# A decay step deferred by half a unit in GLA, and the gates' tanh issued behind the next weight split

## The chip, the core and the metric

One Trainium2 chip, one of its NeuronCores. The metric is the device time of one execution of the whole program in microseconds; lower is better. The program is one launch, hand-scheduled for the five engines: TensorE (PE), VectorE (DVE), ScalarE (ACT), GpSimd (POOL) and SyncE (SP, which issues the weight DMAs).

## What is computed

Two transformer-like blocks in fp32 on a sequence of 512 tokens of width 1024. The first is a hybrid layer: an mLSTM mixer with an output gate, three groups of dilated attention, two merge gates, a SwiGLU FFN. The second has a gated linear attention (GLA), an NSA mixer (compressed, selected and window attention), two merge gates and an FFN. Cut to what the change touches:

```python
# first block
y_a = sigmoid(o_pre) * hm                                # om: 8 column tiles of o_pre
g_a, g_b = split(sigmoid(gate_pre), 2)                   # ga, gb
merged = g_a * (y_a @ w_proj_a) + g_b * (y_b @ w_proj_b) # pa, pb
# second block, GLA (4 heads of 128, chunks of 64)
log_a = log_sigmoid(a_lr @ w_alpha2 + b_alpha) / 16
b = cumsum(log_a)                    # inside each chunk
qe = q * exp(b);  ke = k * exp(-b);  kd = k * exp(b_last - b)
o = ...                              # scores, states over chunks, rms norm
o = o * silu(r)                      # gr: 8 column tiles of r
# merge
mixed = sigmoid(merge_gla) * (o_gla @ w_proj_gla) + sigmoid(merge_nsa) * (o_nsa @ w_proj_nsa)
#                  mg                    pg                    mn                    pn
```

## The kernel before

All projections are cut into 320 "units" in one fixed order (`UNITS`): a unit is a 128-column tile of a weight matrix, up to 8 blocks of 128 x 128 deep. Its weights arrive by a DMA of 512 KB into one of three buffers RAW. For fp32 accuracy each weight is split into a high and a low part: ACT writes WH (L1416, a Copy to fp32r), and then DVE writes WL = RAW - WH (L1695), or POOL does (L2299) where the unit's index is odd and its name is in `BUSY_DVE` (`lo_on_pool`). PE then makes 24 matmuls of 512 columns (L1043 to L1045: high x high, high x low, low x high for each of 8 blocks), about 5.4 us for a unit. WH and WL have three buffers too, so the split of unit u+3 may start when PE is done with unit u.

The order is written out by hand in Python functions that every engine runs with its own class (`Sync`, `Tensor`, `Scalar`, `Vector`, `Pool`), so each engine's instructions come in the order of the same calls:

- `ahead(e, i)`, at a unit's start, issues `split(i + 2)` and `load(i + 5)`.
- `unit(e, i)`: `ahead`, half the products, `flush`, the other half, `flush`, `evict`. `Fill` does the same by quarters (`quarter`; a flush after the second and the fourth) and puts the quarters between the steps of an attention stage: in NSA 96 quarters of the 24 units mg, pg and mn are spread over 28 items, about two of them ahead of an item's scaling and one behind it. Between an item's quarters and the next stand `ask` (PE's scores L1325 or L1337; DVE's L2191 and maximum L2198; ACT's Exps L1614), the output of the item before (PE L1369) and the turn (PE's transposes L1347, ACT's L1625 and DVE's L2252 copies).
- `evict(e, i)`: DVE scales the unit's sum by the row norm (`scaled`, L1723; for gk L1804 and L1806, for gq L1796, for pg L1751). For the gates om, ga, gb, mg, mn (L1438) and gr (L1441) ACT then applies tanh in place or to `th2`. It appends the unit to the list `e.later`.
- `flush(e)` takes each entry of `e.later` once: for a gate DVE turns tanh into the sigmoid (L1852, an SBUF to SBUF TENSOR_SCALAR) or into silu (L1863, for gr); for token-ordered tiles (gv, gk and others) PE transposes the evicted tile (L1108) and DVE copies it out (L1882).

A GLA head's decay is also worked off through `e.later`, as `("decay", h, p)`: p = 0 is the cumulative sum on DVE (L2089) and two Exps on ACT (L1581, L1582); p = 1 four DVE instructions (L2093, L2095, L2099, L2100) and an Exp (L1585); p = 2 one DVE multiply (L2103). Decay 0 starts in the flush in the middle of gr1, decay 1 in that of gv2, decay 2 in that of gv4 and decay 3 in that of gk2. gq waits for "eb" and gk for "enb" and "ekd" of its head. Between heads stands `gla_turned` (PE: scores L1248, transposes L1286 of the head before, updates L1261; DVE: masked copy L2113, gated products L2144, states L2123 and L2126), then `gla_outs` and `gla_scaled` (L2135). `final_norm` (L2107) is one DVE instruction in each of 8 flushes from gv4 on. The order of GLA's units is gr0, gr1, gq0, gk0, gv2, gv3, gq1, gk1, gv4, gv5, gq2, gr2, gr3, gk2, gv6, gv7, gq3 and so on.

DVE, ACT and PE each work strictly in their own order, so an instruction that waits holds all that stand behind it on its engine.

Of the kernel before, what the change touches and what calls it, by code (L numbers as in the profile page):

```python
# [46 lines left out]
def unit_order():  # L47
# [58 lines left out]
    for j in range(8):  # L106
# [8 lines left out]
UNITS = unit_order()  # L115
AT = {(n, j, k0): i for i, (n, j, k0, nk) in enumerate(UNITS)}
PARTS = {"qm": 2, "km": 2, "vm": 1, "om": 1, "va": 1, "ga": 1, "gb": 1, "pb": 1, "small2": 1, "gk": 1, "gv": 1,
         "gr": 1, "vs": 1, "vw": 1, "mg": 1, "mn": 1, "pn": 1}
TOKENS = ("vm", "va", "gk", "gv", "vs", "vw", "small2")
SB = [2, 3, 4]  # L120
OB = 5
# [48 lines left out]
class Order:  # L170
# [3 lines left out]
    def __init__(self):  # L174
        self.ring, self.taken, self.turn = [0, 1, 2, 3], 0, 0
        self.holder, self.bank, self.before, self.later = {}, {}, {}, []
        self.turns_apart = False

    def hold(self, bank, *key):
        self.bank[key], self.before[key] = bank, self.holder.get(bank)  # L180
# [10 lines left out]
    def none(self, *a):  # L191
        pass

    start = load = split = products = evict = after = fold = spread = none
    ones = gates_1 = gates_2 = bias_vector = store_vectors = gate_columns = none
    spread_max = scores = weights = numerators = normed = gated = split_ya = none
    enter_attention = load_bias = attention_scores = attention_softmax = attention_turn = attention_out = none
# [47 lines left out]
            flush_all(self.e)  # L245


def flush(e, turns=True):

    for _ in range(len(e.later)):  # L250
        what, i, part = e.later.pop(0)
        if what == "unit":
            name = UNITS[i][0]
            if name in TOKENS and part == 1:
                if not turns:
                    e.later.append((what, i, part))
                    continue
                e.turn_bank("tokens", i)
            e.after(i, part)
            if part < PARTS.get(name, 1):  # L260
                e.later.append(("unit", i, part + 1))
        elif what == "decay":
            e.decay(i, part)
            if part < 2:
                e.later.append(("decay", i, part + 1))
        elif what == "log_sigmoids":
            e.log_sigmoids_end()
            e.decay(0, 0)
            e.later.append(("decay", 0, 1))
        elif what == "yg":  # L270
            e.split_yg(i)
        elif what == "final":
            e.final_norm(i)
            if i < 7:
                e.later.append(("final", i + 1, 1))
# [7 lines left out]
def ahead(e, i):  # L283
    if i + 2 < len(UNITS):
        e.split(i + 2)
    if i + 5 < len(UNITS):
        e.load(i + 5)

# [9 lines left out]

def evict(e, i):
    e.evict(i)  # L300
    if UNITS[i][0] in PARTS or UNITS[i][:1] + UNITS[i][2:3] == ("down", 16):
        e.later.append(("unit", i, 1))

# [426 lines left out]
def build(nc, xT_d, wst_d, con_d, col_d, relb_d, oh_d, wa2_d, w1_d, w2_d, out_d, scr_d):  # L730
# [6 lines left out]
    with ExitStack() as ctx:  # L737
# [28 lines left out]
        def at(*name):  # L766
            return reached[name] if counted else reached.get(name, (None, 0))
# [615 lines left out]
        class Scalar(Order):  # L1383
# [43 lines left out]
            def two_spreads(s):  # L1427
# [2 lines left out]
                t = A.activation(R1, PS[:, s.bank["spread", "n4"], :], ACT.Copy, scale=1.0)  # L1430
                t.then_inc(*act_done["norm"].next("free", "spread", "n4"))

            def evict(s, i):
                name, j, k0, nk = UNITS[i]
                if name in ("om", "ga", "gb", "mg", "mn"):
                    act.wait_ge(*at("free", "sum", i))
                    x = gate_tile(i)
                    A.activation(x, x, ACT.Tanh, scale=0.5).then_inc(*act_done["attn"].next("tanh", i))  # L1438
                elif name == "gr":
                    act.wait_ge(*at("free", "sum", i))  # L1440
                    t = A.activation(th2, rr[:, j % 2 * 512:j % 2 * 512 + 512], ACT.Tanh, scale=0.5)  # L1441
                    t.then_inc(*act_done["attn"].next("tanh", i))
                elif name == "small2":
                    act.wait_ge(*at("free", "sum", i))
                    t = A.activation(gts[0:24, :], gts[0:24, :], ACT.Tanh, scale=0.5)
                    t.then_inc(*act_done["attn"].next("tanh", i))
                elif name == "out":
                    act.wait_ge(*at("free", "sum", i))
                    s.scaled_hi("h2", AH, j, XT[:, j, :], col("ffn_g", j))
                    s.square("n2", j, XT[:, j, :])  # L1450
                elif name in ("gate", "gate2"):
                    act.wait_ge(*at("free", "sum", i))
                    x = ffn_tile(name, j, 0)
                    A.activation(x, x, ACT.Silu, scale=1.0).then_inc(*act_done["ffn"].next("silu", i))  # L1454
                elif name in ("up", "up2"):
                    x, X, a = ("f", HH, j // 8 * 8) if name == "up" else ("f2", AH, j // 8 * 8)
                    act.wait_ge(*at("free", "sum", i))
                    t = A.activation(X[:, j - a, :], ffn_tile(name, j, 2), ACT.Copy, scale=1.0)
                    t.then_inc(*act_done["ffn"].next(f"{x}{a}", "hi", j - a))
                elif name == "out2":  # L1460
                    act.wait_ge(*at("unit", i))
                    s.square("post2", j, PS[:, s.bank["sum", i], :])
                elif name == "down2" and k0 == 16:
                    act.wait_ge(*at("free", "sum", i))
                    s.square("fpost2", j, OT2[:, j, :])
# [1052 lines left out]
```

## Time and profile before

| | us |
|---|---|
| median of 3 runs | 2014.05 |
| lowest, highest | 2012.61, 2015.61 |
| the profiled execution's own time | 2014.84 |
| its span | 2013.0 |
| PE matmul busy | 1958.1 |
| DVE, ACT, POOL busy | 1045.6, 634.3, 273.9 |

The span runs from the first instruction to the last of the profiled execution. A row of the trace gives start and duration in us, the engine, the source line and the operation, what is written and read, the number of merged instructions and, in square brackets, how long the engine stood idle before it and whose work ended that.

### The profile page before, as it was taken

To read this page: it belongs to the slowest core of one execution; us is meant where nothing else is said; L and a number is where in the kernel's file an instruction comes from. 1 tells how busy PE (TensorE), PEld (TensorE's weight loads), DVE (VectorE), ACT (ScalarE), POOL (GpSimd) and SP (SyncE) were. 2 spreads that over 40 slices of the span, in tenths; PEclk is the share of its full clock that TensorE was granted. 3 is DMA by queue.
4 is the path that set the end of the run, shared out by engine and by line. 5 is a ranking of instruction groups with operands and counts; after the bars stand their busy time and mean duration, and the time that the engine had idled before them with its cause. 6 is when DMAs were issued, how large, how long until landed. Compare 5 with 4: busy or idle time off the path is not lost.

```text
span 2013.0 us, 23621 instructions
## 1 busy us (share of the span) xinstructions
PE 1958.1 (97%) x9642; PEld 1589.3 (79%) x9642; DVE 1045.6 (52%) x1464; ACT 634.3 (32%) x1054; POOL 273.9 (14%) x174
## 2 busy tenths in 40 slices
PE   7999999999999999999999999999999999999997
PEld 5778888888887888888888777877777878888885
DVE  5676643344455744344344766656676544344344
ACT  4333322233333432132234322224444343222222
POOL 1112120011111111010013000111111131011012
PEclk9999999999999999999999999999999989999998
DMA  4222224232311332322223112321111313322221
GB/s 159 81 68 74 84 84 115 84 101 68 94 53 48 120 95 95 105 94 94 94 87 105 60 66 70 100 83 54 55 62 41 119 52 104 105 95 95 94 89 68
DMA packets 52589, 171.81 MB, mean 85 GB/s; under 512 B 5896, under 2 KB 9424, under 8 KB 52481
## 3 DMA queue, kind: packets, MB, share of 16 engines
q1 hardware_dynamic: 51616, 169.08, 26.2%
q8 instruction: 77, 1.26, 0.3%
q10 hardware_dynamic: 864, 1.21, 0.2%
q14 instruction: 32, 0.25, 0.0%
HBM read 168.06 MB, written 2.21 MB: 85 GB/s over the span
## 4 chain that ended last, share of the span: by engine, by line
PE 86%; DVE 9%; ACT 2%; issue 1%; POOL 0%; DMA 0%; SPq 0%; DVEq 0%; ACTq 0%
PE PS L1043 25%; PE PS L1045 25%; PE PS L1044 25%; DVE WL L1695 1%; PE PS L1347 1%; PE PS L1148 1%; PE PS L1325 1%; PE PS L1163 1%; PE PS L1369 1%; PE PS L1186 1%; PE PS L1108 1%; PE PS L1195 1%; PE PS L1209 1%; DVE AR L1723 1%; DVE HL L1686 1%
## 5 line engine op out<-in xcount | busy, mean ns | idle before, releaser
L1043 PE MATMUL PS<-HH,WH 128*128 128x512 f32 x1368 | 542.3, 396 | 16.3 <-DVE WL L1695 10.6
L1045 PE MATMUL PS<-HH,WL 128*128 128x512 f32 x1368 | 535.9, 392 | 0.0
L1044 PE MATMUL PS<-HL,WH 128*128 128x512 f32 x1368 | 535.3, 391 | 0.0
L1416 ACT ACTIVATE WH<-RAW 128x1024 fp32r<-128x1024 f32 (+2 forms) x320 | 325.9, 1019 | 400.8 <-PE PS L1045 400.2
L1695 DVE TENSOR_TENSOR WL<-RAW,WH 128x1024 fp32r<-128x1024 f32 (+2 forms) x258 | 319.1, 1237 | 229.5 <-ACT WH L1416 227.4
L1043 PE MATMUL PS<-AH,WH 128*128 128x512 f32 x1096 | 433.9, 396 | 2.3 <-DVE WL L1695 1.8
L1045 PE MATMUL PS<-AH,WL 128*128 128x512 f32 x1096 | 428.7, 391 | 0.0
L1044 PE MATMUL PS<-AL,WH 128*128 128x512 f32 x1096 | 428.5, 391 | 0.0
L1043 PEld LDWEIGHTS PS<-HH,WH 128*128 128x128 f32 x1368 | 259.0, 189 | 72.5 <-DVE WL L1695 11.3
L1045 PEld LDWEIGHTS PS<-HH,WL 128*128 128x128 f32 x1368 | 258.6, 189 | 55.1
L1044 PEld LDWEIGHTS PS<-HL,WH 128*128 128x128 f32 x1368 | 259.1, 189 | 52.4
L1043 PEld LDWEIGHTS PS<-AH,WH 128*128 128x128 f32 x1096 | 207.1, 189 | 48.4 <-issue 5.7
L2299 POOL TENSOR_TENSOR WL<-RAW,WH 128x1024 fp32r<-128x1024 f32 (+1 forms) x62 | 140.8, 2271 | 757.3 <-ACT WH L1416 757.3
L1045 PEld LDWEIGHTS PS<-AH,WL 128*128 128x128 f32 x1096 | 206.9, 189 | 43.8
L1044 PEld LDWEIGHTS PS<-AL,WH 128*128 128x128 f32 x1096 | 207.2, 189 | 41.4
L1723 DVE TENSOR_TENSOR AR<-PS,RB 128x512 f32<-128x512 f32 (+1 forms) x141 | 101.3, 718 | 230.0 <-PE PS L1045 222.6
L2329 POOL TENSOR_TENSOR AR<-AR,RB 128x512 f32<-128x512 f32 x44 | 57.0, 1296 | 573.6 <-ACT AR L1454 573.6
L1454 ACT ACTIVATE AR<-AR 128x512 f32<-128x512 f32 x44 | 27.8, 632 | 159.1 <-DVE AR L1723 159.1
L1773 DVE TENSOR_TENSOR AR<-AR,PS 128x512 f32<-128x512 f32 x44 | 30.2, 687 | 71.0 <-PE PS L1045 65.6
L1614 ACT ACTIVATE AR<-AR 128x128 f32<-128x128 f32 (+3 forms) x64 | 35.4, 554 | 93.0 <-DVE AR L2198 93.0
L1541 ACT ACTIVATE AR<-AR 128x256 f32<-128x256 f32 (+1 forms) x64 | 31.0, 485 | 87.8 <-DVE AR L1997 87.8
L2290 POOL TENSOR_TENSOR AR<-AR 128x512 f32<-128x512 f32 x30 | 41.2, 1383 | 126.4 <-ACT AR L1408 126.4
(241 smaller groups left out, 1419.6 us busy)
## 6 DMA issues: line engine op xcount, KB each, us to landing
RAW<-wst SPq DMA_DIRECT2D x288, 512.0 KB, 3.4
RAW<-wst SPq DMA_DIRECT2D x16, 384.0 KB, 2.9
RAW<-wst SPq DMA_DIRECT2D x16, 256.0 KB, 2.5
XT<-xT SPq DMA_DIRECT2D x3, 512.0 KB, 7.2
AR<-scr SPq DMA_DIRECT2D x16, 64.0 KB, 4.1
AR<-scr SPq DMA_DIRECT2D x8, 128.0 KB, 4.8
AR<-w SPq DMA_DIRECT2D x2, 512.0 KB, 3.7
out<-XT SPq DMA_DIRECT2D x4, 256.0 KB, 2.1
```

The source lines that it names most:

```text
L1043: T.matmul(out, wh, XH[:, k, :], start=k == 0, stop=False)
L1044: T.matmul(out, wh, XL[:, k, :], start=False, stop=False)
L1045: m = T.matmul(out, wl, XH[:, k, :], start=False, stop=k == nk - 1)
L1416: t = A.activation(WH[:, i % NW, 0:n], RAW[:, i % NR, 0:n], ACT.Copy, scale=1.0)
L1541: t = A.activation(P, P, ACT.Exp, bias=ST[hp % 2][:, x, 0, b, i:i + 1], accum_out=ST[hp % 2][:, x, 1, b, i:i + 1])
L1614: t = A.activation(P, P, ACT.Exp, bias=NST[x][:, 0, hd, m:m + 1], accum_out=NST[x][:, 1, hd, m:m + 1])
L1695: t = V.tensor_tensor(WL[:, i % NW, 0:n], RAW[:, i % NR, 0:n], f(WH[:, i % NW, 0:n]), ALU.subtract)
L1723: return V.tensor_tensor(dst, src, rb, ALU.mult)
L1773: V.tensor_tensor(p, ffn_tile(name, j, 1), src, ALU.mult).then_inc(*bank_read.next(*free))
L2290: t = G.tensor_tensor(acc, acc, sums(norm, n), ALU.add)
L2299: t = G.tensor_tensor(WL[:, i % NW, 0:n], RAW[:, i % NR, 0:n], f(WH[:, i % NW, 0:n]), ALU.subtract)
L2329: t = G.tensor_tensor(ffn_tile(name, j, 1), ffn_tile(name, j, 0), RB, ALU.mult)
```

## The change

Two things. First, `decay` entries with p = 1 are put back into the list as `("decay_on", h, 1)`, which the next flush only turns into `("decay", h, 1)`; p = 2 likewise. So each further step of a decay comes a full unit behind the one before and not half a unit. Second, `evict` no longer issues the tanh of a gate; it notes the unit in `e.fresh`, and `settle` issues it either in the next `ahead`, behind the split, or at the head of the next `flush`, whichever comes first. small2's tanh stays where it was.

```diff
--- before.py
+++ after.py
@@ -116,6 +116,7 @@
 AT = {(n, j, k0): i for i, (n, j, k0, nk) in enumerate(UNITS)}
 PARTS = {"qm": 2, "km": 2, "vm": 1, "om": 1, "va": 1, "ga": 1, "gb": 1, "pb": 1, "small2": 1, "gk": 1, "gv": 1,
          "gr": 1, "vs": 1, "vw": 1, "mg": 1, "mn": 1, "pn": 1}
+GATES = ("om", "ga", "gb", "mg", "mn", "gr")
 TOKENS = ("vm", "va", "gk", "gv", "vs", "vw", "small2")
 SB = [2, 3, 4]
 OB = 5
@@ -174,7 +175,7 @@
     def __init__(self):
         self.ring, self.taken, self.turn = [0, 1, 2, 3], 0, 0
         self.holder, self.bank, self.before, self.later = {}, {}, {}, []
-        self.turns_apart = False
+        self.turns_apart, self.fresh = False, None
 
     def hold(self, bank, *key):
         self.bank[key], self.before[key] = bank, self.holder.get(bank)
@@ -191,7 +192,7 @@
     def none(self, *a):
         pass
 
-    start = load = split = products = evict = after = fold = spread = none
+    activate = start = load = split = products = evict = after = fold = spread = none
     ones = gates_1 = gates_2 = bias_vector = store_vectors = gate_columns = none
     spread_max = scores = weights = numerators = normed = gated = split_ya = none
     enter_attention = load_bias = attention_scores = attention_softmax = attention_turn = attention_out = none
@@ -245,8 +246,17 @@
             flush_all(self.e)
 
 
+def settle(e):
+
+    if e.fresh is not None:
+        e.activate(e.fresh)
+    e.fresh = None
+
+
 def flush(e, turns=True):
 
+
+    settle(e)
     for _ in range(len(e.later)):
         what, i, part = e.later.pop(0)
         if what == "unit":
@@ -262,11 +272,13 @@
         elif what == "decay":
             e.decay(i, part)
             if part < 2:
-                e.later.append(("decay", i, part + 1))
+                e.later.append(("decay_on", i, part + 1))
+        elif what == "decay_on":
+            e.later.append(("decay", i, part))
         elif what == "log_sigmoids":
             e.log_sigmoids_end()
             e.decay(0, 0)
-            e.later.append(("decay", 0, 1))
+            e.later.append(("decay_on", 0, 1))
         elif what == "yg":
             e.split_yg(i)
         elif what == "final":
@@ -283,6 +295,7 @@
 def ahead(e, i):
     if i + 2 < len(UNITS):
         e.split(i + 2)
+    settle(e)
     if i + 5 < len(UNITS):
         e.load(i + 5)
 
@@ -298,6 +311,8 @@
 
 def evict(e, i):
     e.evict(i)
+    if UNITS[i][0] in GATES:
+        e.fresh = i
     if UNITS[i][0] in PARTS or UNITS[i][:1] + UNITS[i][2:3] == ("down", 16):
         e.later.append(("unit", i, 1))
 
@@ -1430,17 +1445,19 @@
                 t = A.activation(R1, PS[:, s.bank["spread", "n4"], :], ACT.Copy, scale=1.0)
                 t.then_inc(*act_done["norm"].next("free", "spread", "n4"))
 
+            def activate(s, i):
+                name, j, k0, nk = UNITS[i]
+                act.wait_ge(*at("free", "sum", i))
+                if name == "gr":
+                    t = A.activation(th2, rr[:, j % 2 * 512:j % 2 * 512 + 512], ACT.Tanh, scale=0.5)
+                    t.then_inc(*act_done["attn"].next("tanh", i))
+                else:
+                    x = gate_tile(i)
+                    A.activation(x, x, ACT.Tanh, scale=0.5).then_inc(*act_done["attn"].next("tanh", i))
+
             def evict(s, i):
                 name, j, k0, nk = UNITS[i]
-                if name in ("om", "ga", "gb", "mg", "mn"):
-                    act.wait_ge(*at("free", "sum", i))
-                    x = gate_tile(i)
-                    A.activation(x, x, ACT.Tanh, scale=0.5).then_inc(*act_done["attn"].next("tanh", i))
-                elif name == "gr":
-                    act.wait_ge(*at("free", "sum", i))
-                    t = A.activation(th2, rr[:, j % 2 * 512:j % 2 * 512 + 512], ACT.Tanh, scale=0.5)
-                    t.then_inc(*act_done["attn"].next("tanh", i))
-                elif name == "small2":
+                if name == "small2":
                     act.wait_ge(*at("free", "sum", i))
                     t = A.activation(gts[0:24, :], gts[0:24, :], ACT.Tanh, scale=0.5)
                     t.then_inc(*act_done["attn"].next("tanh", i))
```

## Rows read from the trace of the kernel before

**Rows 1.** The page, part 1: busy time of each engine, share of the span, instructions.

```profile
PE 1958.1 (97%) x9642; PEld 1589.3 (79%) x9642; DVE 1045.6 (52%) x1464; ACT 634.3 (32%) x1054; POOL 273.9 (14%) x174
```

**Rows 2.** PE in order of time: its waits from 1110 to 1230 us.

```profile
1135.90 0.47 PE L1043 MATMUL PS<-AH,WH 128*128 128x512 f32 x1 [1.79 <-DVE WL L1695]
...
1140.03 0.63 PE L1108 MATMUL PS<-C,AR 128*128 128x128 f32 x4 [1.15 <-DVE AR L1806]
...
1178.44 0.66 PE L1286 MATMUL PS<-C,AR 128*128 128x128 f32 x4 [1.73 <-DVE AR L2113]
...
1188.92 0.63 PE L1108 MATMUL PS<-C,AR 128*128 128x128 f32 x4 [1.17 <-DVE AR L1723]
...
1216.94 0.63 PE L1108 MATMUL PS<-C,AR 128*128 128x128 f32 x4 [1.78 <-DVE AR L1806]
```

**Rows 3.** Busy time by stretch: PE, PEld, DVE, ACT, POOL, then granted clock, DMA share, GB/s.

```profile
1150.00:1200.00 50.00, 47.10 (x237) 37.80 (x237) 34.71 (x53) 11.49 (x20) 1.20 (x2) 1.00 0.23 74
```

**Rows 4.** ACT and DVE in order of time, around gr1 to gk0.

```profile
1129.06 0.63 ACT L1581 ACTIVATE AR<-AR 128x512 f32<-128x512 f32 x1 [5.28 <-DVE AR L2089]
...
1133.38 2.94 ACT L1416 ACTIVATE WH<-RAW 128x1024 fp32r<-128x1024 f32 x3
...
1134.53 1.23 DVE L1695 TENSOR_TENSOR WL<-RAW,WH 128x1024 fp32r<-128x1024 f32 x1 [1.72 <-ACT WH L1416]
...
1139.21 0.68 DVE L1806 TENSOR_TENSOR AR<-PS,AR 128x512 f32<-128x512 f32 x1
```

**Rows 5.** DVE in order of time, around gv4 and gv5.

```profile
1174.52 0.17 DVE L2093 COPY AR<-AR 128x8 f32<-128x8 f32 x1 [0.57 <-ACT AR L1582]
...
1177.67 0.71 DVE L2113 COPY_PREDICATED AR<-C,PS 128x512 f32<-128x512 int32 x1
...
1188.10 0.68 DVE L1723 TENSOR_TENSOR AR<-PS,RB 128x512 f32<-128x512 f32 x1
```

**Rows 6.** DVE in order of time, at gk2.

```profile
1213.63 0.17 DVE L2093 COPY AR<-AR 128x8 f32<-128x8 f32 x1 [1.22 <-ACT AR L1582]
...
1216.12 0.68 DVE L1806 TENSOR_TENSOR AR<-PS,AR 128x512 f32<-128x512 f32 x1
```

**Rows 7.** DVE and POOL at the same time, NSA stage.

```profile
1529.71 2.35 POOL L2299 TENSOR_TENSOR WL<-RAW,WH 128x1024 fp32r<-128x1024 f32 x1 [20.23 <-ACT WH L1416]
...
1529.88 2.78 DVE L2212 TENSOR_SCALAR AR<-AR,GT 128x384 f32<-128x384 f32 x2
```

**Rows 8.** DVE, ACT, POOL and PE around the gate mg6.

```profile
1452.93 0.42 DVE L1852 TENSOR_SCALAR VT<-VT 128x512 f32<-128x512 f32 x1
...
1454.41 1.05 ACT L1416 ACTIVATE WH<-RAW 128x1024 fp32r<-128x1024 f32 x1
...
1454.47 1.00 DVE L2212 TENSOR_SCALAR AR<-AR,GT 128x512 f32<-128x512 f32 x2
...
1455.60 2.36 POOL L2299 TENSOR_TENSOR WL<-RAW,WH 128x1024 fp32r<-128x1024 f32 x1 [18.16 <-ACT WH L1416]
...
1457.32 1.09 PE L1347 MATMUL PS<-C,AR 128*128 128x128 f32 x8
...
1464.41 1.11 PE L1347 MATMUL PS<-C,AR 128*128 128x128 f32 x8
```

**Rows 9.** DVE and ACT around the gate mg5.

```profile
1433.35 0.63 ACT L1438 ACTIVATE VT<-VT 128x512 f32<-128x512 f32 x1
...
1433.43 1.38 DVE L2212 TENSOR_SCALAR AR<-AR,GT 128x256 f32<-128x256 f32 x4
```

**Rows 10.** PE's waits at mn3 and mn4.

```profile
1522.70 1.09 PE L1369 MATMUL PS<-AR 128*64 128x128 f32 x16 [1.18 <-DVE AR L2252]
...
1532.32 0.94 PE L1347 MATMUL PS<-C,AR 128*128 128x128 f32 x6 [1.73 <-DVE AR L2212]
```

**Rows 11.** DVE and PE around the gate gb1.

```profile
605.52 0.43 DVE L1852 TENSOR_SCALAR AR<-AR 128x512 f32<-128x512 f32 x1 [0.70 <-ACT AR L1438]
...
609.04 0.65 PE L1195 MATMUL PS<-C,AR 128*128 128x128 f32 x4 [1.07 <-DVE AR L2049]
```

## The prediction

> **What bounds the kernel now.** I read the page's first part, then PE's own waits in order of time, then, around each wait, what DVE and ACT did just before it. TensorE is busy 97% of the span [rows 1], so almost all of the 2013 us is matmul work that this change leaves alone. What can move is the time in which PE stands, and the change touches two stretches of it: the GLA projections (1110 to 1230 us), and the places where a gate unit ends while DVE is short of time (gb in the attention, mg and mn in the NSA stage). In GLA there are five waits of PE: 1.79, 1.15, 1.73, 1.17 and 1.78 us, 7.62 us in all [rows 2]. All five end with a DVE instruction, and in none is PE waiting for the work of that instruction alone: DVE reaches it late. The granted clock there is 1.00 (2.4 GHz) in spite of such waits [rows 3], so I price them as time and put no clock change on them.
>
> **GLA, first two waits (gr1's tanh).** Before, ACT runs tanh of gr1 and only behind it the three splits of the next weights; the tanh waits for DVE's eviction of gr1, which stands behind the whole first decay on DVE. So the split of gv2 starts at 1133.38, DVE's WL at 1134.53, and PE, which ends gk0 at about 1134.1, waits until 1135.90 [rows 2, 4]. Changed: at the end of gr1 DVE has no decay step left (it comes one flush later), so the eviction follows the scan at about 1129.1 (scan end: 0.63 us of Exp start it at 1129.06), ACT splits gv2 right behind the two Exps at 1130.2, 1.04 us long, and WL ends at about 1132.6, ahead of need. The 1.79 goes. What is late next is gk0's eviction: DVE still has WL gv2, decay step 1 (2.0), the gate, gq0's eviction, WL gv3, step 2 and L1804, L1806 to do. Added up from 1131.35 in the start to start distances of this stretch (WL 1.14, 512 wide ones 0.60, L2093 0.08): 1.14+0.08+3x0.60+0.60+0.60+1.14+0.60+0.60+0.68 = 7.24, so L1806 ends at 1138.6 instead of 1139.9 [rows 4]. PE's transposes of gk0 start at 1138.7, not 1140.03: it waits some 2.1 there, and the two waits of 2.94 become 2.1 net of the shift. **-1.33.** No further ACT table load comes with the tanh of gr0 moving behind the Ln: one load there simply precedes the tanh and not the Exp.
>
> **GLA, decay of head 2.** Before, step 1 (four DVE instructions, 1174.52 to 1176.48) stands in the flush at the end of gv4, ahead of the eviction and of L2113, for which PE waits 1.73 [rows 2, 5]. Changed, it comes 2.7 us of PE later, in the middle of gv5. DVE then evicts gv4 as soon as PE is done and L2113 ends about 0.5 ahead of need. **-1.73.** But the four instructions now stand ahead of gv5's eviction (L1723 at 1188.10), for which PE already waits 1.17. The order of DVE's work from L2113 on, with step 1 in it: L2113 at 1174.1, one L2144 at once, the other at 1176.1 behind PE's transposes, states to 1180.3, WL 1.2, step 1 2.0, one final norm 0.67, token copy 0.6, two L1686 1.2, a final norm 0.66: the eviction starts at 1186.45 and ends at 1187.15, so PE goes on at 1187.25 instead of 1188.92. The gain so far was 3.06 and is 1.67 now: **+1.39** given back.
>
> **GLA, decay of head 3.** The same step stands ahead of L1804 and L1806, with 1.22 idle in front of it while ACT makes the Exps [rows 6]. Moved behind them it leaves L1806 ending about 1.4 ahead of need: **-1.78**; from there the step falls beside gv6, where DVE keeps up. Sum in GLA: -1.33-1.73+1.39-1.78 = **-3.45**. Bounds: -1.3 if each deferral is fully given back at the next eviction, -7.62 if all five waits went.
>
> **The tanh behind the split.** Where DVE makes WL of the unit three on, this is harmless or gains: WL comes up to 0.53 (the start to start distance of a tanh and a split) or a wait for the eviction earlier. Where POOL makes it (all mg, the even mn and gb, the even om), something else decides. DVE's L2212, alone some 0.5 long for 512, took 2.78 for two when POOL's subtraction of 2.35 had just begun [rows 7]. So an SBUF to SBUF TENSOR_SCALAR on DVE that starts beside POOL's WL waits until POOL ends. The gate's own L1852 is of that kind. Before, tanh, then split, then POOL: L1852 was over when POOL began. Changed: split, then tanh 1 us long behind it, and POOL starts 0.14 after the split's end, so L1852 finds POOL at work in nearly every such unit.
> The Trainium skill, SBUF — State Buffer, Who interferes with whom, says that a DVE instruction in a two-port mode or with two SBUF inputs and a GpSimd instruction take an exclusive lock, that the first one has it for its whole length and the other blocks; this speaks against the change, and the 2.78 agrees. If this lock weren't there the NSA terms below would be about 0.
> In mlstm and ga DVE is idle behind the gate op or WL is DVE's, so I count nothing; with that cover gone it would cost at most one POOL length, 2.4, at one place.
> - **mg6** [rows 8]: the eviction closes a portion of work, so ACT runs the Exps of the next item, then the split (1454.41 to 1455.46), and only now tanh, to 1456.0. POOL has started at 1455.60. L1852, which ran at 1452.93, is held until 1457.96 and ends 1458.2; the scaling L2212 behind it gives its first half at 1458.95, and PE's transposes, due at 1457.32, wait **+1.65**. The next item runs DVE, ACT (Exps, split), DVE with WL ahead of the scaling and no room at 1464.41; its scaling comes at 1466.85 where PE is at 1466.06: **+0.85**.
> - **mg5** [rows 9]: tanh at 1433.35 goes, the split starts at 1433.1 and POOL at 1434.3, just ahead of the fourth L2212 (about 1434.4). It is held until 1436.9, PE needs it at 1435.95: **+0.95**; 0 if the fourth still slips in.
> - **mn0, mn2, mn4** [rows 10]: PE waits for DVE already (1.18, 1.73), so nothing hides a held L1852. But at mn4 L2212 is held in any case, and mn1, mn3, mn5 give back 0.53 each. I take **+1.35** for the six; bounds -1.6 (three times 0.53, no hold) and +5.5 (three times 2.36, less 1.6).
> - **gb1** [rows 11]: L1852 at 605.52 is held from about 604.2+2.36 on to 606.75, 0.8 late; L2049 and PE behind it too, of which 0.35 comes back since L2054 is no longer held: **+0.45**; bounds 0 and 1.6.
> - mg0, mg2, mg4: L1852 held about 2, but PE's next need lies 3 or more behind. mg1, mg3, mg7: it comes after POOL. 0.
> Sum: 2.50+0.95+1.35+0.45 = **+5.25**.
>
> **The sum.** -3.45+5.25 = +1.80 on the profiled execution's 2014.84 (span 2013.0), 2016.6. That execution is 0.8 above the median 2014.05, so I put **2015.8** beside the median. A difference within 0.2% (4.0 us) is about what a measurement of this kernel can't tell from no change.
>
> **The rivals.**
> (1) The gate ops find room: PE's slack or an earlier arrival of DVE takes up the holds. Then GLA's -3.45 stands with some +0.5: 2011.1. If GLA's DVE had more room too (the 1.17 goes with the rest) it is -7.62, 2006.4. For: several gate ops lie right behind an eviction. Against: rows 7 and the order at mg6.
> (2) Slower, by the port between DVE and POOL. Place: mg5, mg6 and mn. It decides from where POOL's start lies ahead of L1852 and L2212 with less than 2.4 of room behind them. If each of the three mn costs half a POOL length more, +3.5, with GLA's gain at its lower bound -1.3: 2014.05-1.3+5.25+3.5 = 2021.5. With one of these two only: 2018 to 2019.
> (3) The change doesn't do what it says: deferring a step shifts DVE's load from one eviction to the next. For head 2 that is what I expect in large part; if for head 3 as well, GLA gives -1.7 and the time is 2017.6.
>
> **How the numbers follow.** Chances: forecast and (3), 2013 to 2018, 0.57; (1) 0.23, of which 0.14 below 2010.0; (2) 0.20, nearly all above 2018.1, and 0.03 of the forecast's edge with it. So faster 0.14, same 0.63, slower 0.23. The range holds 8 in 10: from 2010.0 to 2019.8.
>
> **What would show it.** In the changed profile: no wait of PE for WL at gv2, and the wait at gk0's transposes near 2 us; none for L2113; a longer one, 2 to 2.6, at gv5's transposes; none at gk2's. ACT's L1416 ahead of the tanh in each gate unit. L1852 with durations or waits near 2 us in mg and mn, and new waits of PE for L2212 near mg5 and mg6. I would be wrong if L1852 stayed at 0.42 throughout, or if the wait at gv5 stayed near 1.2.

## The result: slower by 0.24%, and the profile after

The changed kernel takes 2019.01 us (median of 10 runs, 2018.33 to 2021.03), the kernel before 2014.55 us beside it (10 runs, 2012.61 to 2015.61): ratio 1.0024, 95% interval 1.0016 to 1.0033. Forecast were 2015.8 us, 1.8 slower, and no difference that a measurement can tell. The time lies in the range of 2010.0 to 2019.8, but only 0.8 below its upper end, and the direction is the one forecast; what does not fit is the size: the loss is 4.5 us, over the 4.0 that I had taken for no change.

The profiled execution took 2019.03 us (span 2017.2), 4.2 more than the one before. Its first part, as [rows 1]:

```profile
PE 1958.3 (97%) x9642; PEld 1589.9 (79%) x9642; DVE 1069.8 (53%) x1464; ACT 633.6 (31%) x1054; POOL 273.8 (14%) x174
```

PE, ACT and POOL are as before; DVE has 24.2 us more of busy time with the same 1464 instructions, so some of its instructions lasted longer. It is the sigmoid step of the gates: the durations of its 40 instructions add up to 42.9 us (L1869), to 18.2 in the kernel before (L1852).

**How I took the two traces apart.** PE issues the same 9642 matmuls in the same order in every kernel of this study, so they can be paired one by one. For each pair the start to start distance differs by two things: by the idle time in front of the matmul (a wait), or without idle time (the matmul before it ran slower or faster, that is, the clock). A "slow stretch" below is a run of matmuls of 512 columns that take 0.63 us each where they otherwise take 0.39, at a granted clock near one half. Summed by stretch, changed kernel minus kernel before, in us:

| stretch of the kernel before | what lies there | waits | clock |
|---|---|---|---|
| 0 to 600 | first block | -0.13 | +0.44 |
| 600 to 620 | gb1 | +0.99 | +1.58 |
| 620 to 1105 | rest of block 1 | +0.01 | -1.64 |
| 1105 to 1138 | gr0 to gk0 | +0.08 | -3.18 |
| 1138 to 1170 | behind gk0 | +1.87 | +1.64 |
| 1170 to 1200 | gv4, gv5 | -0.46 | -0.05 |
| 1200 to 1240 | gk2 | -1.78 | -0.18 |
| 1440 to 1480 | mg6, mg7 | +2.61 | +0.27 |
| 1480 to 1560 | mn | +0.89 | +1.58 |
| rest | | 0.00 | -0.22 |
| sum | | +4.08 | +0.24 |

**GLA.** PE in order of time, its waits from 1130 to 1200 us, as [rows 2]:

```profile
1133.92 0.47 PE L1058 MATMUL PS<-AH,WH 128*128 128x512 f32 x1 [1.87 <-DVE WL L1712]
...
1139.94 0.63 PE L1123 MATMUL PS<-C,AR 128*128 128x128 f32 x4 [3.02 <-DVE AR L1823]
1140.64 0.54 PE L1059 MATMUL PS<-AL,WH 128*128 128x512 f32 x1
1140.99 0.63 PE L1060 MATMUL PS<-AH,WL 128*128 128x512 f32 x1
1141.41 0.63 PE L1058 MATMUL PS<-AH,WH 128*128 128x512 f32 x1
...
1189.94 0.63 PE L1123 MATMUL PS<-C,AR 128*128 128x128 f32 x4 [2.43 <-DVE AR L1740]
```

There are three waits where there were five; the two of 1.73 and 1.78 (L2113 and gk2) are gone. But a product matmul takes 0.63 behind the wait of 3.02 where it takes 0.39 otherwise. The granted clock by stretch (columns as in [rows 3]), first two stretches of the changed kernel, then the same two of the kernel before:

```profile
1115.00:1120.00 5.00, 5.00 (x25) 4.16 (x25) 3.06 (x5) 3.08 (x4) 0.00 (x0) 1.00 0.00 0
...
1140.00:1145.00 5.00, 5.00 (x19) 4.06 (x20) 2.71 (x4) 1.15 (x2) 0.00 (x0) 0.66 0.55 179
```

```profile
1115.00:1120.00 5.00, 5.00 (x14) 3.84 (x14) 1.95 (x3) 3.58 (x5) 0.00 (x0) 0.53 0.00 0
...
1140.00:1145.00 5.00, 4.97 (x30) 4.30 (x32) 3.78 (x6) 1.38 (x3) 0.00 (x0) 1.00 0.65 203
```

The slow stretch lies at 1115 before and at 1140 after. At 1115 it cost 3.2 us of PE's time, but PE then waited for DVE at gv2 anyway, and waited that much less; at 1140, behind the wait for gk0's eviction, nothing absorbs it.

**The gates.** ACT, DVE, POOL and PE around mg6, as [rows 8]:

```profile
1453.48 1.05 ACT L1431 ACTIVATE WH<-RAW 128x1024 fp32r<-128x1024 f32 x1
1454.43 0.62 ACT L1456 ACTIVATE VT<-VT 128x512 f32<-128x512 f32 x1
...
1454.68 2.34 POOL L2316 TENSOR_TENSOR WL<-RAW,WH 128x1024 fp32r<-128x1024 f32 x1 [18.57 <-ACT WH L1431]
...
1455.08 2.22 DVE L1869 TENSOR_SCALAR VT<-VT 128x512 f32<-128x512 f32 x1 [3.00 <-ACT VT L1456]
...
1458.02 1.11 PE L1362 MATMUL PS<-C,AR 128*128 128x128 f32 x8 [1.56 <-DVE AR L2229]
...
1465.89 1.11 PE L1362 MATMUL PS<-C,AR 128*128 128x128 f32 x8 [0.78 <-DVE AR L2229]
```

The order is now split, then tanh, and POOL starts 0.15 behind the split's end. L1869 (L1852 before, 0.42 there) lasts 2.22 and ends 0.28 behind POOL, and PE's transposes have two waits that were not there. At mn4, as [rows 10]:

```profile
1532.90 2.35 POOL L2316 TENSOR_TENSOR WL<-RAW,WH 128x1024 fp32r<-128x1024 f32 x1 [21.23 <-ACT WH L1431]
...
1533.31 2.22 DVE L1869 TENSOR_SCALAR AR<-AR 128x512 f32<-128x512 f32 x1 [0.68 <-ACT AR L1456]
...
1536.17 1.23 PE L1362 MATMUL PS<-C,AR 128*128 128x128 f32 x6 [2.39 <-DVE AR L2229]
```

And at gb1, as [rows 11]:

```profile
604.48 2.36 POOL L2316 TENSOR_TENSOR WL<-RAW,WH 128x1024 fp32r<-128x1024 f32 x1 [10.02 <-ACT WH L1431]
...
605.72 1.40 DVE L1869 TENSOR_SCALAR AR<-AR 128x512 f32<-128x512 f32 x1 [0.70 <-ACT AR L1456]
...
610.22 0.66 PE L1210 MATMUL PS<-C,AR 128*128 128x128 f32 x4 [2.06 <-DVE AR L2066]
```

All 40 instructions of the line, from the view of one source line (duration ns least, median, greatest); 18 of them last over 1 us, one of the 40 in the kernel before:

```profile
L1869 DVE TENSOR_SCALAR AR<-AR x32: 417/428/2571, 74.0 to 1555.5; 128x512 f32<-128x512 f32 x32
L1869 DVE TENSOR_SCALAR VT<-VT x8: 411/1319/2250, 1347.4 to 1476.0; 128x512 f32<-128x512 f32 x8
```

### The profile page after: what moved, and what is told of

The parts are those of the page before. It is cut to its first block, busy times and chain, and to the rows that moved or that the text cites. A ratio compares the mean times of both kernels' runs of the same rounds, so it can differ in the third digit from the quotient of the medians.

```text
span 2017.2 us, 23625 instructions
## 1 busy us (share of the span) xinstructions
PE 1958.3 (97%) x9642; PEld 1589.9 (79%) x9642; DVE 1069.8 (53%) x1464; ACT 633.6 (31%) x1054; POOL 273.8 (14%) x174
## 4 chain that ended last, share of the span: by engine, by line
PE 85%; DVE 10%; ACT 3%; issue 1%; POOL 0%; DMA 0%; SPq 0%; DVEq 0%; ACTq 0%
PE PS L1058 25%; PE PS L1060 25%; PE PS L1059 25%; DVE WL L1712 1%; PE PS L1163 1%; PE PS L1178 1%; PE PS L1362 1%; PE PS L1201 1%; PE PS L1123 1%; ACT WH L1431 1%; PE PS L1210 1%; PE PS L1224 1%; ACT AR L1631 1%; PE PS L1384 1%; DVE AR L1740 1%
```

## The experiments

Twelve kernels in three sets of four. Theory at the start: the two halves act apart, GLA gains some 2 us, the tanh behind the split costs 5.3 in NSA and 1.0 at gb1 because DVE's sigmoid step then meets POOL. All at a glance; "waits" and "clock" are the sums of the pairing above for the one profiled execution, which lies 4.5 us off the median in e6, 4.1 in e10 and 1.8 in e9 and e12; "mean clock" is that of all runs of the kernel; the ratio is close to that of the means, which is not that of the medians where a kernel's runs lie in groups (e3, e6). The two columns are to be read together where DVE sets the end of a wait: a PE that ran faster ahead of it waits the longer. At gv2 it waits 1.79 in the kernel before and 5.0 in e6 and e7, which leave that place alone and ran there without a slow stretch of 3.2:

| kernel | median us | ratio to before, 95% | waits | clock | mean clock |
|---|---|---|---|---|---|
| before | 2014.4 | | | | 0.9880 |
| changed | 2019.01 | 1.0024 (1.0016 to 1.0033) | +4.08 | +0.24 | 0.9874 |
| e1_decay_only | 2014.82 | 0.9997 (0.9988 to 1.0006) | -2.69 | +2.98 | 0.9868 |
| e2_tanh_only | 2019.57 | 1.0026 (1.0016 to 1.0036) | +4.51 | +0.09 | 0.9879 |
| e3_only_gr_late | 2014.10 | 0.9992 (0.9984 to 1.0001) | -3.03 | +2.48 | 0.9872 |
| e4_gate_wl_on_dve | 2014.61 | 1.0000 (0.9991 to 1.0009) | +0.72 | -0.65 | 0.9877 |
| e5_gb_late | 2017.59 | 1.0016 (1.0007 to 1.0024) | +0.58 | +2.30 | 0.9876 |
| e6_mg6_late | 2017.27 | 1.0008 (0.9999 to 1.0017) | +4.91 | -6.56 | 0.9889 |
| e7_head3_only | 2012.50 | 0.9990 (0.9981 to 0.9999) | +0.72 | -2.18 | 0.9878 |
| e8_mn_late_dve | 2010.95 | 0.9977 (0.9968 to 0.9986) | -4.80 | +1.08 | 0.9880 |
| e9_mn_dve_early | 2014.05 | 0.9994 (0.9985 to 1.0002) | +0.29 | -2.88 | 0.9875 |
| e10_head3_mn | 2010.73 | 0.9977 (0.9968 to 0.9986) | -1.42 | -6.58 | 0.9876 |
| e11_late_if_dve | 2010.12 | 0.9977 (0.9966 to 0.9987) | -4.40 | +0.43 | 0.9886 |
| e12_gb_early | 2017.43 | 1.0010 (1.0001 to 1.0019) | +0.18 | +4.53 | 0.9877 |

### First set: each half alone, and POOL taken out

**e1_decay_only**, to the kernel before:

```diff
-                e.later.append(("decay", i, part + 1))
+                e.later.append(("decay_on", i, part + 1))
+        elif what == "decay_on":
+            e.later.append(("decay", i, part))
...
-            e.later.append(("decay", 0, 1))
+            e.later.append(("decay_on", 0, 1))
```

> Only the first half of the change: each further decay step comes one flush later; every tanh is issued in evict as before. My theory: the two halves act apart. The GLA stretch gains about 2 us (the changed kernel had 2.1 there), there is no wait in the attention or the NSA stage that the kernel before lacks, and the time is 2012.5 us, 0.9990 of before. Rival A: GLA's gain needs the late tanh of gr1 (the split of gv2 stands behind it); then the first two waits keep their length and the gain is 1 us or less, 0.9995 or more. Rival B: the slow stretch of the clock in GLA is set by chance, and the gain is the 3.45 forecast, 0.9983.

Measured: 2014.82 us, no difference. By its waits the theory holds: GLA has 2.8 us less of them, with two waits left of five, and nothing is new elsewhere.

```profile
1138.75 0.63 PE L1110 MATMUL PS<-C,AR 128*128 128x128 f32 x4 [2.37 <-DVE AR L1808]
...
1188.71 0.63 PE L1110 MATMUL PS<-C,AR 128*128 128x128 f32 x4 [2.43 <-DVE AR L1725]
```

The time does not follow. Eight matmuls of 512 run slow behind the wait of 2.37 (+1.6), so that GLA gives 1.7. And eight transposes near 1620 us that run at full clock in the kernel before do not here (first the kernel before, then e1):

```profile
1619.85 1.16 PE L1083 MATMUL PS<-C,RC 128*128 128x128 f32 x8 [1.35 <-POOL RC L2310]
```

```profile
1617.75 2.07 PE L1085 MATMUL PS<-C,RC 128*128 128x128 f32 x8 [1.35 <-POOL RC L2312]
```

The stretch around them gives 1.2 back, and one with the same transposes at 1998 us another 1.0. Nine of its 11 runs lie between 2014.5 and 2015.2, at a mean clock of 0.986 to 0.987, the other two at 2009.8 and 2009.9, at 0.990; no run of the kernel before was below 2012.3. So the gain is there in waits, and in the profiled run the clock took it; the eight runs beside it have the same time and mean clock.

**e2_tanh_only** is the changed kernel with the two lines of e1 taken back.

> Only the second half: all decay steps as before, the tanh of every gate behind the next split. My theory: the holds of DVE behind POOL's WL cost 5.3 us in the NSA stage and 1.0 at gb1, as in the changed kernel, with the same waits at mg6 (1.6) and the item behind it (0.8); in GLA the split of gv2 no longer waits for gr1's eviction, which is worth up to 1.3. Time 2019.5 us, 1.0025 of before (1.0031 if GLA gains nothing). The waits of 1.73, 1.17 and 1.78 in GLA stay. Rival: the NSA loss comes from another source than the late tanh (a later arrival of the whole stage), then it is absent here and the time is 2013 to 2015.

Measured: 2019.57 us, ratio 1.0026, as the theory has it: +0.99 at gb1, +2.62 at mg6 and +0.88 in mn, and in GLA the wait at gk0's transposes stays 1.15 while PE, early at gv2, waits 3.34 there. I had expected all of 1.73, 1.17 and 1.78 to stay: 1.74 and 1.53 do, the 1.17 at gv5 is gone, behind a slow stretch (+1.4) that brings PE there later. GLA as a whole gives 1.6 here, 1.7 in e1 and 2.1 with both halves, so its gains don't add up. The second half alone is as slow as the whole change. The rival, a later arrival of the stage, is not settled by this run, whose stage arrives as late as in the changed kernel (mg6's transposes at 1458.48 and 1458.02); e6 settles it.

**e3_only_gr_late**: the changed kernel, in `evict`:

```diff
-    if UNITS[i][0] in GATES:
+    if UNITS[i][0] in ('om', 'ga', 'gb', 'mg', 'mn'):
+        e.activate(i)
+    elif UNITS[i][0] in GATES:
         e.fresh = i
```

> The changed kernel, but only the tanh of gr comes behind the split; om, ga, gb, mg and mn have theirs in evict as before. My theory: it keeps the gain of GLA (about 2 us) and has neither the wait at gb1 nor those of NSA: 2012.4 us, 0.9989 of before, and faster than the changed kernel by some 6.5 us, and within 0.5 us of the kernel with the decay steps alone or up to 1.3 us faster than it. L1871's instructions on VT tiles are 0.42 us long throughout. Rival: NSA loses by its phase (GLA done earlier) also without the late tanh; then 2017 us or more.

Measured: 2014.10 us, ratio 0.9992, 4.9 faster than the changed kernel. None of the waits at gb1 and in NSA is there (difference 0.01 and 0.01), GLA has 3.2 us less of them. As in e1 the clock takes most of it back (+1.6 at 1140, +1.3 near 1620, +0.9 at 1999), so the time is 1.7 above what I expected.

**e4_gate_wl_on_dve**: the changed kernel, with one more condition:

```diff
 def lo_on_pool(i):
+    if UNITS[i - 3][0] in ("mg", "mn", "gb"):
+        return False
     return i % 2 == 1 and i > 1 and UNITS[i][0] in BUSY_DVE
```

> The changed kernel, but the WL of the units three behind mg, mn and gb is made by DVE, never by POOL, so that no sigmoid step of these gates can find POOL at work; the tanh stays late. DVE has some 1.2 us more work for each such unit. If the hold behind POOL is the cause of the NSA loss: no sigmoid step of mg and mn above 0.5 us, the wait at mg6 falls from 1.56 to 0.2 or 0.5, NSA's loss falls from 5.3 to 1 to 3 us (what remains is DVE's longer work), and the time is 2014 to 2017 us, 1.0002 to 1.0012. Rival: the loss comes from the order on ACT and DVE (the tanh 0.5 to 1 us later) and not from POOL; then DVE's added work comes on top and it is 2020 us or more, 1.0027 or more.

Measured: 2014.61 us, ratio 1.0000, 4.4 less than the changed kernel, though DVE got more to do. DVE around mg6, and PE's waits behind it:

```profile
1454.91 1.23 DVE L1714 TENSOR_TENSOR WL<-RAW,WH 128x1024 fp32r<-128x1024 f32 x1 [2.55 <-ACT WH L1433]
1456.05 0.42 DVE L1871 TENSOR_SCALAR VT<-VT 128x512 f32<-128x512 f32 x1
...
1457.18 1.11 PE L1364 MATMUL PS<-C,AR 128*128 128x128 f32 x8 [0.45 <-DVE AR L2231]
...
1465.06 1.11 PE L1364 MATMUL PS<-C,AR 128*128 128x128 f32 x8 [0.78 <-DVE AR L2231]
```

The tanh comes as late as in the changed kernel, the sigmoid step lasts 0.42, and the wait falls from 1.56 to 0.45. So the held sigmoid step is POOL's doing, and with it most of the loss. Not all of the waits go: 0.45 and 0.78 stay at mg6 and the item behind it, 1.42 at gb1 with its slow stretch. At mg6 and at gb1 DVE's own WL (1.23) now stands ahead of the sigmoid step, and this run can't tell its cost from that of the late tanh; e11, which has none of these waits, leaves both out. That DVE's WL costs something shows at another place (+1.0 of waits between 1340 and 1440 us).

### Second set: single gates, a single head, and a first better version

**e5_gb_late**: the kernel before, with the `e.fresh` branch for the gb units alone.

> The kernel before, with the tanh of the eight gb units alone behind the split. Theory: PE's wait at gb1 is 2.06 instead of 1.07, and behind it eight matmuls of 512 columns run at the lower clock (about +1.6), as in the changed kernel; the slow matmuls before the GLA stage and at its start are fewer (-1.6 and -3.2), but DVE sets the end of the GLA projections' first waits, so that only the +1.1 of DVE's late start stays: 2015.5 us, 1.0005 of before, and up to 2017 if one more slow stretch comes. Rival: the slow stretch at 611 us has nothing to do with this wait; then there is none, the stage is 1.0 later and the slow stretches at 1097 and 1114 us stay as they were: also about 2015.5, but with another trace.

Measured: 2017.59 us, ratio 1.0016, more than either expected. The wait of 2.05 is there, and so is the slow stretch: the granted clock from 610 to 615 us is 0.67 in e5 and 1.00 in the kernel before.

```profile
610.00:615.00 5.00, 4.75 (x17) 3.98 (x18) 2.18 (x4) 2.13 (x7) 0.00 (x0) 0.67 0.01 3
```

```profile
610.00:615.00 5.00, 5.00 (x24) 4.21 (x25) 2.14 (x4) 1.89 (x6) 0.00 (x0) 1.00 0.31 102
```

Two more slow stretches came in GLA that the trace of the kernel before has not: 6 matmuls behind the wait at gv2 (3.37 here, 1.79 before) and 7 behind the one for L2113 (1.74 here, 1.73 before), +1.4 and +1.6. But the waits behind these two, 1.15 at gk0 and 1.17 at gv5, are gone for it, so GLA as a whole is only 0.3 longer than in the kernel before. Nor does gb1's slow stretch stay in the sum: 1.6 come back near 1097 us, as in the changed kernel. What is left of this trace's loss is the wait of 1.0 and 2.4 of clock near 1620 and 1999 us. And it is one of only three runs at a mean clock of 0.986; the other eight have 0.988 or 0.989, like the kernel before, and six of them take 2017.6 to 2018.1. So the edit makes one wait 1.0 us longer and the kernel 3.2 slower, and the traces don't show where the other 2 go in most runs.

**e6_mg6_late**: the kernel before, with the `e.fresh` branch for `UNITS[i][:2] == ("mg", 6)` alone.

> The kernel before, with the tanh of one gate alone, mg6, behind the split. Theory: the sigmoid step of mg6 takes over 2 us beside POOL, PE's waits of 1.56, 0.78 and up to 0.3 appear behind it and nowhere else, +2.4 to +2.7 with a further +0.3 of the clock: 2017.1 us, 1.0013 of before. Rival: PE's waits at mn3 and mn4, for DVE too, shrink by as much, since PE arrives later: 2014.5, 1.0000.

Measured: the median is 2017.27, but the interval of the ratio (0.9999 to 1.0017) takes in no difference: its runs lie at 2012.5 to 2012.8 (3), 2015.5 to 2015.8 (2) and 2017.3 to 2018.7 (6). The profiled one is of the first kind; it had no slow stretch between 620 and 1130 us at all. As to waits it is plain:

```profile
1454.65 1.11 PE L1362 MATMUL PS<-C,AR 128*128 128x128 f32 x8 [1.55 <-DVE AR L2229]
1462.52 1.11 PE L1362 MATMUL PS<-C,AR 128*128 128x128 f32 x8 [0.78 <-DVE AR L2229]
```

Both waits come from the tanh of this one gate, 2.33 us, and the waits in mn are what they were before (1.18, 1.74, 0.81): nothing is absorbed, the rival is out. So is that of e2: PE is 2.7 us earlier here than in the kernel before (1454.65, 1457.32) and waits all the same, and in e3 and e5 it does not wait.

**e7_head3_only**: the kernel before, with `"decay_on" if i == 3 else "decay"`.

> The kernel before, with the decay steps of head 3 alone put off by a flush each. Both theories expect the wait of 1.78 at gk2 gone and no other wait changed, so the stages behind arrive 1.8 us earlier. Theory: what the clock takes back hangs on the arrival at the slow stretches near 1620 and 1999 us, as in the kernel with all decay steps put off (2.2 us there); the time is 2013.8 to 2014.6, 0.9997 to 1.0001. Rival: the clock took it back because of the longer waits of 2.37 and 2.43 in GLA, which are not there; then the gain stays, 2012.6 us, 0.9991.

Measured: 2012.50 us, ratio 0.9990. The wait of 1.78 at gk2 is gone, none has come behind it, and those of head 2 (1.74 and 1.17) are what they were. The time is the rival's; but the runs spread from 2009.3 (3 of them) over 2012 to 2013 (4) to 2015.3 (4), so what decides whether the clock takes the gain back I can't tell from it. Its trace has the slow transposes of e1 at 1620 us, and not those at 1999.

**e8_mn_late_dve**: the changed kernel, tanh of om, ga, gb and mg early as in e3, mn's late, and the condition of e4 for mn alone.

> A version meant to beat both kernels: all decay steps put off, the tanh of gr and mn behind the split, that of om, ga, gb and mg in evict as before, and the WL of the units three behind mn made by DVE. Theory: waits as in the kernel where only gr is late up to 1480 us (3.0 less than before in GLA) and as in the one with these WL on DVE from there on (1.7 less in mn): the stretch up to 1600 us is 5 us shorter than before, 3.5 with the slow matmuls at 1140 us. With some 2 us given back to the clock near 1620 and 1999 us: 2012.5 us, 0.9990. Rival: the clock gives back all: 2014.4, 1.0000; or nothing behind 1600 us: 2010.5, 0.9981.

Measured: 2010.95 us, ratio 0.9977 (0.9968 to 0.9986): faster than both kernels. The waits are near what I had computed: -3.2 in GLA, -1.73 in mn. The clock took 1.6 behind gk0 and 0.8 near 1620 us, none at 1999.

### Third set: where the late tanh pays

**e9_mn_dve_early** is e8 with mn's tanh in evict.

> The kernel e8_mn_late_dve (decay steps put off, tanh of gr and mn late, WL behind mn on DVE; 2010.95 us), with the tanh of mn in evict as before; only its WL stays on DVE. Theory: of the 1.73 us of waits that e8 loses in the mn units, 0.8 at mn4 comes from DVE's scaling no longer standing behind POOL, and is kept; the rest comes from WL starting 0.5 us earlier where the tanh stands behind the split, and is lost: waits from 1480 to 1560 us down by 0.5 to 1.0, the time 2011.9 us, 0.9981 of before. Rival: all of it comes from WL on DVE: 2010.9, 0.9977.

Measured: 2014.05 us, ratio 0.9994. Waits from 1480 to 1560 us: -0.02 against -1.73 in e8. WL on DVE alone is worth nothing, less than my theory had (0.5 to 1.0 kept); the whole gain needs the late tanh, and the rival is out.

**e10_head3_mn** is e8 with the steps of heads 0 to 2 half a unit apart, as before.

> The kernel e8_mn_late_dve, with the steps of head 3 alone put off and those of heads 0, 1 and 2 half a unit apart as before. Theory: gr1's late tanh alone brings the split of gv2 forward and the wait at gk0's transposes stays at 1.15 with no slow stretch at 1140 us behind it (as in the kernel with the late tanh alone); head 2 keeps 1.73 and 1.17 in place of one wait of 2.43, 0.5 worse; head 3 gives its 1.78. GLA ends 3.0 to 3.5 us ahead of the kernel before (e8: 2.5): 2010.3 us, 0.9974. Rival: the late tanh without the deferral gains nothing here: GLA ends 1.8 ahead, 2011.7, 0.9981.

Measured: 2010.73 us, ratio 0.9977, the same as e8. GLA by its waits and clock: 3.35 at gv2, where PE came early, 1.13 at gk0's transposes, 1.74 and 1.14 for head 2, none at gk2, and no slow matmul in the whole of GLA, as the theory has it. The profiled execution took 2006.63 us, with hardly a slow matmul from 60 to 1600 us, so its sum over the whole kernel is no measure of the edit.

**e11_late_if_dve**: the changed kernel, in `evict`:

```diff
-    if UNITS[i][0] in GATES:
+    if UNITS[i][0] in GATES and lo_on_pool(i + 3):
+        e.activate(i)
+    elif UNITS[i][0] in GATES:
         e.fresh = i
```

> The changed kernel, but with the tanh behind the split only where DVE makes the WL three units on (gr, odd mn and gb, odd om and so on); where POOL makes it, the tanh is in evict as before. Theory: only POOL makes the late tanh costly, so none of the waits of 1.56, 0.78, 0.28 at mg6 and none above 1.07 at gb1 is there, the sigmoid step of mg is 0.42 us long throughout, and the NSA stage is 0 to 1 us shorter than in the kernel with gr's tanh alone late (2014.10 us): 2013.1 to 2014.1 us, 0.9987 to 0.9992, some 5 us faster than the changed kernel. Rival: the late tanh costs by its order too: some waits of the changed kernel in mn (0.44, 0.73, 0.73) are there, and it is 2015 us or more, 1.0003.

Measured: 2010.12 us, ratio 0.9977 (0.9966 to 0.9987), the lowest median of all, 3 us below the lower end of what I expected. The sigmoid steps of mg from the view of the line, and PE's waits in mn:

```profile
L1871 DVE TENSOR_SCALAR VT<-VT x8: 408/417/587, 1344.7 to 1470.3; 128x512 f32<-128x512 f32 x8
```

```profile
1518.95 1.09 PE L1386 MATMUL PS<-AR 128*64 128x128 f32 x16 [0.48 <-DVE AR L2271]
...
1528.57 0.94 PE L1364 MATMUL PS<-C,AR 128*128 128x128 f32 x6 [1.74 <-DVE AR L2231]
...
1536.07 1.30 PE L1364 MATMUL PS<-C,AR 128*128 128x128 f32 x8 [0.29 <-DVE AR L2231]
```

Against [rows 10]: 1.18 has become 0.48 and the third wait 0.29 (0.79 before), where DVE makes WL; the one at mn4, where POOL makes it, is unchanged. The 40 sigmoid steps add up to 18.2 us again. With the order chosen by who makes WL, a change that cost 4.5 us gains 4. Waits in mn fall by 1.28, more than the 1 us at most that I had given them, and in this trace nothing is lost near 1620 and 1999 us.

**e12_gb_early** is the changed kernel with gb's tanh in evict.

> The changed kernel, with the tanh of the gb units in evict as before. Theory: the wait at gb1 is 1.07 again and the slow stretch at 611 us is gone; the kernel with gb alone late was 3.2 us slower than the kernel before, 1.0 of it this wait and the rest clock. If this adds up, the changed kernel gains 1 to 3 us: 2016.0 to 2018.0, 1.0008 to 1.0018 of before. Rival: the wait is hidden by DVE's later bound in GLA, and the time stays at 2019.0, 1.0024.

Measured: 2017.43 us, ratio 1.0010: 1.6 below the changed kernel, inside what the theory gave. The wait at gb1 is 1.08 and no matmul is slow behind it. The 3.2 us that gb's late tanh costs in e5 are not all here. Its profiled execution took 2019.27 us, the longest of the 11.

## Why the prediction was off, step by step

**GLA's waits were right.** Forecast: -1.33, -1.73, +1.39, -1.78. In the trace, against the 1.14 us by which PE already comes later: the transposes of gk0 at -1.23, the wait for L2113 gone (-1.73), the wait at gv5's transposes 2.43 in place of 1.17 (+1.27), the one at gk2 gone (-1.78). The chain of DVE that I added up ends at L1823 as forecast. At gv2 I had expected no wait and found 1.87, but not because WL was late: it ended at 1133.78, which is the forecast 1132.6 and the late arrival. PE was 3.2 us early, since it ran at full clock where it had been slow before.

**The step that failed** in GLA is "so I price them as time and put no clock change on them". [Rows 3] showed the clock at 1.00 in a stretch with a wait of 1.73; the prediction reads no stretch from 1097 to 1120, where it was down to 0.53, nor does it ask what hides that. One slow stretch of 7 matmuls came behind the wait of 3.02 (+1.64) with nothing behind it to absorb it. So GLA gave -2.07, not -3.45, and behind gb1 and mn4 the same unpriced term comes to 1.58 each.

**gb1 was mis-sized.** Forecast +0.45: L1852 to end at 606.75, with 0.35 coming back at L2054. It ended at 607.12, 0.97 late after allowing for 0.2 of later arrival; and L2054 (L2071 in the changed kernel), 1.04 long before, is 1.05 long now, when POOL was done at 606.84, long ahead of it. It is 1.05 in e4 too, where POOL has no WL near it. So POOL never held it, and nothing comes back; why it is longer than its neighbours (0.68) no run shows. The wait grew by 0.99, and 8 slow matmuls behind it cost another 1.58.

**NSA was near the sum and wrong in its parts.** mg6: forecast 1.65 and 0.85, measured 1.56 and 0.78, and 0.28 at a third item; e6 shows that they come from this gate alone. mg5: forecast 0.95, measured 0; the fourth L2229 slipped in ahead of POOL, the case that I named. DVE and POOL there:

```profile
1432.50 1.38 DVE L2229 TENSOR_SCALAR AR<-AR,GT 128x256 f32<-128x256 f32 x4
1434.00 0.48 DVE L2235 SCALAR_TENSOR_TENSOR AR<-C,PS 128x124 f32<-128x124 f32 x2
1434.51 0.41 DVE L2241 TENSOR_REDUCE AR<-AR 128x8 f32<-128x248 f32 x1
1434.96 1.42 DVE L2243 TENSOR_TENSOR AR<-AR 128x248 f32<-128x248 f32 x1
...
1433.56 2.55 POOL L2316 TENSOR_TENSOR WL<-RAW,WH 128x1024 fp32r<-128x1024 f32 x1 [13.20 <-ACT WH L1431]
```

POOL starts at 1433.56 and ends at 1436.11. L2235 (PSUM input) and the reduction run at their usual length beside it; L2243, with both inputs in SBUF, is held and ends at 1436.38, 0.27 behind POOL, as L1869 does at mg6 and mn4; and POOL itself, begun while the scalings ran, takes 2.55 for 2.35. The Trainium skill, SBUF — State Buffer, Who interferes with whom, says that only DVE instructions with two SBUF inputs or in a two-port mode contend with GpSimd, and that the first to issue blocks the other; by these rows the trace agrees. mn: forecast +1.35, measured +0.89 of waits and +1.58 of clock behind the wait of 2.39.

**The sum.** Forecast +1.80; the pairing gives 4.08 + 0.24 = +4.3. Of the 2.5 between them GLA is 1.4 (the slow stretch behind gk0, less some 0.2 elsewhere), gb1's wait 0.5, NSA 0.5 (4.80 forecast, 5.35 measured), and 0.1 the stretches that no edit touches. gb1's slow stretch nets to nothing here: the 1.58 was evened out by -1.64 at slow matmuls from 1097 to 1103 us that this execution has fewer of.

**What of this was luck.** The time lies in the range because that was wide: the sum was 2.5 us short. It also falls at the upper end of the 2018 to 2019 that rival (2) gives for one of its two conditions, but neither came about as stated: mn cost 1.1 more than forecast, not 3.5, and by the clock, not by the holds, and GLA's gain fell to 2.1, not 1.3.

**The rivals.** (1), that the gate steps find room, is out by e2 and e6. (2), that DVE and POOL hold each other up, is the mechanism that makes it slower, and my own sum had it too: e4 takes POOL away and 4.4 us go, e11 leaves the order to who makes WL and 8.9 us go. Its price in mn was lower in waits than I gave it (0.9 for 1.35 and up), but the clock raised it. (3), head 3 given back, is out by e7, which loses the wait at gk2 and has no new one behind it. What I had weighed too little is that the parts of a gain aren't alike: a wait taken away may be filled by the clock, while a wait added can bring a slow stretch with it.

## What to carry to other kernels

Where one engine can hold another up (here a DVE step of 0.42 us took 2.22 beside POOL's WL), the place of a small instruction on a third engine (here a tanh on ACT) decides whether DVE is over before POOL starts: move it only where POOL has no part, as `lo_on_pool(i + 3)` does in e11. Price a wait with the stretch of clock that may follow it, ask what further on absorbs that stretch, and read the granted clock of every stretch that a moved wait may fall in, those where PE is slow and nothing shows it above all. Where half a change gains and the other half loses, run the halves: here each half's effect could be read from its waits, and one condition kept the gain of both.

## What the runs showed of the hardware

**A wait of PE and the clock behind it.** At gb1 the same place was run with different waits. With 1.07 or 1.08 us (the kernel before and e1, e3, e6 to e12: 10 traces) no matmul behind it was slow; with 1.42 (e4), 2.05 (e2, e5) and 2.06 (changed kernel) 5 to 8 matmuls of 512 columns took 0.63 instead of 0.39, 1.4 to 1.6 us in all, each time. So with the wait the clock level fell from 2.4 to 1.2 GHz. It did not add up over the kernel: in these four traces the stretch near 1097 us, slow in the kernel before, gives 1.6 back. That stretch comes and goes by itself as well (as before in e1, e3, e7, e8, e11 and e12, 1.6 less in e9, 3.3 less in e6 and e10). At mn4 it is the same: slow behind 2.38 to 2.41 (changed kernel, e2, e12), and not behind 1.28 to 1.74 (the other 11). In GLA it is not a matter of the one wait: behind 2.43 or 2.44 at gv5 the clock fell in e12 and not in the other 7 kernels that have it, behind 1.74 at L2113 in e2 and e5 and not in the kernel before, e6, e7 or e10. What else decides there, these runs don't settle.

**A program whose time comes in groups.** Most kernels here have runs 2 to 5 us apart with the same code: e1 at 2009.8 and 2014.8, e7 at 2009.3, 2012.4 and 2015.3, e10 from 2005.7 to 2011.3. In most kernels a faster run has a higher mean granted clock (0.990 or 0.991 against 0.986 or 0.987); e5 is the exception. Between the traces, one of each kernel, slow stretches come and go near 1097, 1115, 1620 and 1999 us, at instructions that no edit moves. That it is these by which the runs of one kernel differ too is likely and not shown, since only one run of each was traced. With groups this far apart, a difference of 2 us between two kernels is not safely told from a few runs each; a single wait can be followed from trace to trace (gb1's 1.07 or 1.08 in 10 of them).
